# A 64-byte shift of the weight tiles against the activation tiles in SBUF, in a two-layer hybrid decoder trunk

## The chip, the cores and the metric

The kernel runs on one core of one Trainium2 chip. The metric is the device time of one execution, in microseconds (us). It is computed in float32: every large product is made from float32 operands that are split into a rounded high part and a remainder, so that one product takes three matmuls.

## The reference

One sequence of 512 tokens with 1024 features goes through two layers. Layer 0 mixes tokens with an mLSTM (8 heads), layer 1 with sliding-window attention (16 query heads, 2 key heads, window 128). Each mixer is followed by a gated MLP of width 2816.

```python
for i in range(DEPTH):                                   # 2 layers
    z = rmsnorm(h, norm_mix_pre[i])
    z = mlstm_mixer(...) if i % 2 == 0 else swa_sink_mixer(...)
    h = h + rmsnorm(z, norm_mix_post[i])
    z = conv_ffn(rmsnorm(h, norm_ffn_pre[i]), f_w_up[i], f_conv_w[i], f_conv_b[i], f_w_down[i])
    h = h + rmsnorm(z, norm_ffn_post[i])

def conv_ffn(h, w_up, conv_w, conv_b, w_down):
    gate, val = jnp.split(h @ w_up, 2, axis=-1)
    gate_c = conv_b + sum(conv_w[j] * pad(gate)[:, j:j + S] for j in range(3))
    return (jax.nn.silu(gate_c) * val) @ w_down
```

## The kernel before

**Operands.** Weights come from HBM by SyncE's queue into `raw` (4 slots of 128 x 1024 float32). ScalarE rounds a slot into `w_hi` (8 slots), VectorE writes the remainder `raw - w_hi` into `w_lo` (8 slots). Activations are kept the same way, as `act_hi` and `act_lo`. A product is then three matmuls that add up in PSUM: high by high, high by low, low by high. For each of them TensorE first loads one operand (128 x 128, the stationary one) and then streams the other (256 or 512 columns, the moving one). The load for a matmul is made while the matmul before it streams.

Which of the two is the weight depends on the stage. In `project` (lines 1803 to 1811) and in `product` (lines 2054 to 2065) the stationary operand is a weight tile and the moving one an activation. In `v_unit` (1889 to 1891), `out_part` (2000 to 2002) and `down_part` (2094 to 2096) it is the reverse. There the hidden activations of the MLP, also split in two, lie for most of the work in `hid_pair`, which is slot 2 of `w_hi` and `w_lo`; they are stationary, and slots 0 and 1 are moving.

**The MLP's first product in sevens.** Of 22 tiles of the MLP's width, 18 go through a loop in which eight half-size products are replaced by seven (a scheme like Strassen's), on sums of weights and of activations. One pass of the loop handles two tiles (t = 0 and 1); what is done for one tile is called a half pass here, and there are 36 half passes in the kernel, 18 in each layer. A half pass on TensorE is seven products of 12 matmuls with 256 columns, in this order, named by their moving operand:

- `z1a` from `act_hi`/`act_lo`; `t3` from `t_third`; `t2` from `t_early`; `t4` from `t_last`; `t1` from `t_early`; `z2a` and `z2b` from `act_hi`/`act_lo`.

Their stationary operands are forms in `w_hi` and `w_lo`. For the next tile GpSimd makes four sums of raw weights in `sums` (lines 611 to 616; `sums` lies on `w_lo`) as soon as `z2b` of the tile before this one is done (line 610). ScalarE rounds (lines 870, 872, 880), VectorE takes remainders (1517, 1520, 1533). Between the products ScalarE copies parts out of PSUM (line 892), and `t2`, `t4`, `t1` and `z2b` each wait for one of these copies, because they go on in the bank that it reads. `t2` waits for the copy of `z1a`'s result into `u_full`. That copy stands on ScalarE behind the SiLU of the tile before (line 903), and the SiLU waits for the convolution on VectorE (lines 1455, 1459). So four engines hang together in one ring of waits.

**Where the tiles lie.** Tiles are laid down one behind the other in the order in which the program names them, each on the next multiple of 32 bytes. In bytes per partition: `raw` 16384, `w_hi` 32768, `w_lo` 32768, `act_hi` 16384, `act_lo` 16384, `h` 16384, `g_post` and `g_pre` 4096 each, `arena` 65696, `ident` 512, `causal` 512, `ones` 4 (the next tile begins 32 further), `band` 1024, `u_full` 2048, `parts` 3072, `t_last` 8192. `t_early` lies 49152 bytes into `arena`, and `t_third` on `g_post` and `g_pre`. The streamed slices begin at multiples of 512 bytes within their tiles.

`freed(g)` (line 105) gives the count of used weight units for which the writer of unit `g` in a slot has to wait; it has a case of its own for slot 2, because `hid_pair` is kept there.

Of the kernel before, what the change touches and what calls it, by code (L numbers as in the profile page):

```python
# [30 lines left out]
P = 128  # L31
# [8 lines left out]
def trunk(nc, x, x_turned, columns, m_w_in, m_gate_bias, m_w_out, a_w_in, a_sinks, a_w_out,  # L40
          a_b_out, norm_mix_pre, norm_mix_post, norm_ffn_pre, norm_ffn_post, f_w_up, f_w_down, out):
    S, D = x.shape[1], x.shape[2]
# [9 lines left out]
    HALF = 512  # L52
# [19 lines left out]
    G_DOWN = [G_UP[0] + 2 * FT, 0]  # L72
    G_AIN = G_DOWN[0] + FT
    A_UNITS = (QH + 2 * KVH) * DH // P
    PLAIN = 4
    SEVENS = FT - PLAIN
    HT = S // 2
    QW = KT // 2 * P
    assert FT % 2 == 0 and PLAIN == 4
# [6 lines left out]
    SLOT = [0, 1, 2, 3, 7] + [n % 4 for n in range(QK_UNITS - FIRST + V_UNITS + O_UNITS)]  # L86
    FFN_SLOTS = [4 + n % 4 for n in range(2 * PLAIN)]
    FFN_SLOTS += [(0, 1, 6, 7)[n % 4] for n in range(2 * SEVENS)] + [n % 2 for n in range(FT - TAIL)]
    FFN_SLOTS += list(range(4, 4 + TAIL))
# [14 lines left out]

    def freed(g):
        users = [q for q in range(g) if SLOT[q] == SLOT[g]]
        if SLOT[g] == 2 and g > G_DOWN[0]:

            users.append(G_DOWN[0] + FT - TAIL - 1)
        for l in range(2):  # L110
            if g >= G_DOWN[l]:

                users.append(G_DOWN[l] - (1 if SLOT[g] >= 4 else 3))
        return counted(max(users, default=-1))
# [4 lines left out]
    with ExitStack() as ctx:  # L119
        def sb(name, shape, dt=F32):  # L120
            return ctx.enter_context(nc.sbuf_tensor(name, shape, dt))
# [4 lines left out]
        def below():  # L126
            return (nc.sbuf_base + 31) // 32 * 32
# [2 lines left out]


        raw = sb("raw", [P, 4, D])
        w_hi = sb("w_hi", [P, 8, D], F32R)
        w_lo_at = below()
        w_lo = sb("w_lo", [P, 8, D], F32R)
        sums = nc.alloc_sbuf_tensor_at("sums", [P, 2, 8, D // 2], F32, offset=w_lo_at)

        act_hi = sb("act_hi", [P, KT, S], F32R)
        act_lo = sb("act_lo", [P, KT, S], F32R)
        h = sb("h", [P, NB, D])  # L140
# [13 lines left out]
        u_rows = u_full[0:MH]  # L154
        first_part = u_full[:].rearrange("p (b t) -> p b t", b=2)
        parts = sb("parts", [P, 3, S // 2])
        t_last_at = below()
        t_last = sb("t_last", [P, 2, D], F32R)
        t_last_sum = nc.alloc_sbuf_tensor_at("t_last_sum", [P, D], F32, offset=t_last_at + 4 * D)
# [87 lines left out]
        gate_sum = arena[0:40, Q + 7 * HALF:Q + 8 * HALF]  # L247


        hid_pair = [[w[:, 2, j * HALF:(j + 1) * HALF] for w in (w_hi, w_lo)] for j in range(2)]  # L250


        raw_in = [sem(f"raw_in{i}") for i in range(4)]
# [291 lines left out]
        def _(pool):  # L545
# [56 lines left out]
            def weight_sums(l, m, t):  # L602

                up, n = G_UP[l], l * SEVENS + t - PLAIN
                gate, val = raw[:, 2 * t], raw[:, 2 * t + 1]
# [34 lines left out]
        def _(act):  # L640
# [194 lines left out]
            def ffn(l):  # L835
# [58 lines left out]
                def joined_conv(m, t):  # L894

                    n = l * SEVENS + t - PLAIN
                    f = m * 2 + t
# [1455 lines left out]
```

How the kernel before makes its waits and increments, by code:

```python
        @block.sync  # L395
# [7 lines left out]
            def load_free(g):  # L403
                last = [q for q in range(g) if SLOT[q] % 4 == SLOT[g] % 4 and DMAS[q]]
                if last:
                    sp.wait_ge(w_lo_done, counted(last[-1]))
# [12 lines left out]
                load(m, w_k[:, 2 * m:2 * m + 2, 0:HALF], raw[:, m].rearrange("p (k c) -> p k c", k=2))  # L420
            nc.sync.dma_start(g_col[:], columns[:, 0:KT]).then_inc(g_col_in, 16)
            nc.sync.dma_start(raw[:, 0, 0:HALF], m_w_in[0, 0:P, 0:HALF]).then_inc(w_first_in, 16)
            load_turned(1, 2)
            load(0, w_k[:, 1, 0:HALF], raw[:, 0, HALF:])
            for m in range(1, FIRST):
                load_turned(2 * m, 2 * m + 2)
                load_first(m)
            GC = m_w_in.shape[2] - ROWS
            sp.wait_ge(pool_done, 1)
            nc.sync.dma_start(wg[:, :, 0:MH], w_k[:, :, GC:GC + MH]).then_inc(wg_in, 16)
            nc.sync.dma_start(wg[:, :, 32:32 + MH], w_k[:, :, GC + MH:GC + ROWS]).then_inc(wg_in, 16)
            for j in range(2):
# [4 lines left out]
            nc.sync.dma_start(vecs[:], columns[:, KT:]).then_inc(vec_in, 16)  # L438
            for n in range(FIRST, QK_UNITS):
                g = g_qk(n)
                load_free(g)
                load(g, w_k[:, :, n * P:(n + 1) * P], raw[:, SLOT[g] % 4].rearrange("p (k c) -> p k c", k=KT))
            sp.wait_ge(sum_done, KT - 1)
            nc.sync.dma_start(h[:, 0], x[0, 0:P]).then_inc(x_in[0], 16)
            VC = 2 * MH * DK
```

## Time and profile before

| | |
|---|---|
| median of 3 runs | 1062.31 us (1061.8 to 1062.31) |
| the profiled execution | 1061.99 us, of which 1060.2 us are the span shown in the profile |
| TensorE (PE) busy | 1051.5 us, 99% of the span, 6822 matmuls |
| VectorE (DVE), ScalarE (ACT), GpSimd (POOL) busy | 730.1, 531.5 and 271.9 us |
| granted clock of TensorE, mean over the span | 0.999 of 2.4 GHz |
| matmuls on split operands with 256 columns | 3840: 3024 in the sevens (lines 2061 to 2063), 816 in `project` (lines 1808 to 1810) |
| of these 816 | 48 in the mLSTM's last unit, 384 in the attention's projections, 192 at the head of each MLP |
| matmuls on split operands with 512 columns | 2248: 1056 in `down_part`, 504 in `project`, 384 in `out_part`, 192 in `v_unit`, 112 in the first units and gates |

In the rows further down, PE is a matmul and PEld the load of its stationary operand. A matmul's record lasts longer than its share of the pace, since successive matmuls overlap in the array: the pace is read from start to start. In a timeline a row is the start, the length, the engine, the line, the operation and its operands (out<-in); in brackets stands the idle time before it and who ended it.

### The profile page before, as it was taken

The numbers are of one execution on the slowest core, as the hardware profiler recorded it, in microseconds if no ns is written. First come the engines' busy times: TensorE is split into PE (matmuls) and PEld (weight loads), VectorE is DVE, ScalarE is ACT, GpSimd is POOL, SyncE is SP. The second block draws the span as 40 slices with busy tenths as digits, with TensorE's granted clock in tenths as the row PEclk, the third lists the DMA queues.
The fourth block names the chain that finished last, engine by engine and source line by source line (L and its number), as shares of the span: only waits on it lengthen the run. The fifth ranks groups of instructions, "written<-read, shape, count | busy, mean of one in ns | idle before, by whom it ended". The sixth has DMA issues, their size and how long they took to land.

```text
span 1060.2 us, 18750 instructions
## 1 busy us (share of the span) xinstructions
PE 1051.5 (99%) x6822; PEld 943.5 (89%) x6822; DVE 730.1 (69%) x1013; ACT 531.5 (50%) x971; POOL 271.9 (26%) x195
## 2 busy tenths in 40 slices
PE   9999999999999999999999999999999999999997
PEld 8888888898999999988889987789999999988886
DVE  7534579588988988633366577678898898943354
ACT  6511447445565565422355367754566566542242
POOL 1000211004565565100000023300656556400000
PEclk9999999999999999999999999999999999999999
DMA  9342328233343343122272552123234334222232
GB/s 287 108 120 80 100 81 253 48 97 91 89 119 109 88 119 113 55 92 97 99 198 61 133 127 80 21 60 100 64 96 119 100 98 119 79 80 99 99 139 80
DMA packets 154828, 111.18 MB, mean 105 GB/s; under 512 B 35536, under 2 KB 140144, under 8 KB 154784
## 3 DMA queue, kind: packets, MB, share of 16 engines
q1 hardware_dynamic: 153776, 107.41, 34.5%
q0 software_dynamic: 864, 2.92, 0.9%
q8 instruction: 28, 0.46, 0.2%
q10 hardware_dynamic: 144, 0.26, 0.1%
q14 instruction: 16, 0.13, 0.0%
HBM read 106.87 MB, written 2.13 MB: 103 GB/s over the span
## 4 chain that ended last, share of the span: by engine, by line
PE 93%; DVE 4%; SPq 1%; ACT 1%; issue 1%; DMA 0%; DVEq 0%; ACTq 0%
PE ps L2061 11%; PE ps L2063 11%; PE ps L2062 11%; PE ps L2095 8%; PE ps L2096 8%; PE ps L2094 8%; PE ps L1808 6%; PE ps L1810 5%; PE ps L1809 5%; PE ps L2000 2%; PE ps L2002 2%; PE ps L2001 2%; PE ps L1889 1%; PE ps L1890 1%; PE ps L1891 1%; PE ps L2191 1%
## 5 line engine op out<-in xcount | busy, mean ns | idle before, releaser
L1808 PE MATMUL ps<-act_hi,w_hi 128*128 128x256 f32 (+1 forms) x440 | 144.8, 329 | 1.5 <-DVE act_lo L1153 1.4
L1809 PE MATMUL ps<-act_lo,w_hi 128*128 128x256 f32 (+1 forms) x440 | 142.4, 324 | 0.0
L1810 PE MATMUL ps<-act_hi,w_lo 128*128 128x256 f32 (+1 forms) x440 | 142.4, 324 | 0.0
L2061 PE MATMUL ps<-act_hi,w_hi 128*128 128x256 f32 x432 | 122.4, 283 | 0.0
L2062 PE MATMUL ps<-act_lo,w_hi 128*128 128x256 f32 x432 | 122.4, 283 | 0.0
L2063 PE MATMUL ps<-act_hi,w_lo 128*128 128x256 f32 x432 | 122.4, 283 | 0.0
L1604 DVE TENSOR_TENSOR w_lo<-raw,w_hi 128x1024 fp32r<-128x1024 f32 x32 | 39.2, 1225 | 117.0 <-ACT w_hi L952 117.0
L611 POOL TENSOR_TENSOR sums<-raw 128x512 f32<-128x512 f32 x36 | 48.3, 1341 | 262.3 <-PE ps L1810 139.6
L2095 PE MATMUL ps<-w_lo,w_hi 128*128 128x512 f32 x288 | 112.1, 389 | 0.0
L2094 PE MATMUL ps<-w_hi 128*128 128x512 f32 x288 | 112.1, 389 | 0.0
L2096 PE MATMUL ps<-w_hi,w_lo 128*128 128x512 f32 x288 | 112.1, 389 | 0.0
L653 ACT CAST w_hi<-raw 128x1024 fp32r<-128x1024 f32 x66 | 68.1, 1045 | 63.8 <-PE ps L1891 24.7
L952 ACT CAST w_hi<-raw 128x1024 fp32r<-128x1024 f32 x32 | 33.7, 1053 | 121.5 <-PE ps L2096 121.5
L1808 PEld LDWEIGHTS ps<-act_hi,w_hi 128*128 128x128 f32 x440 | 83.7, 190 | 10.5 <-DVE act_lo L1153 1.8
L1103 DVE TENSOR_TENSOR w_lo<-raw,w_hi 128x1024 fp32r<-128x1024 f32 x65 | 78.5, 1219 | 18.8 <-ACT w_hi L653 18.8
L1810 PEld LDWEIGHTS ps<-act_hi,w_lo 128*128 128x128 f32 x440 | 83.7, 190 | 6.7
L1809 PEld LDWEIGHTS ps<-act_lo,w_hi 128*128 128x128 f32 x440 | 83.7, 190 | 6.5 <-issue 0.2
L1533 DVE TENSOR_TENSOR w_lo<-sums,w_hi 128x1024 fp32r<-128x1024 f32 x72 | 87.0, 1211 | 0.0
L880 ACT CAST w_hi<-sums 128x1024 fp32r<-128x1024 f32 x72 | 75.7, 1054 | 22.3 <-POOL sums L616 22.3
L2062 PEld LDWEIGHTS ps<-act_lo,w_hi 128*128 128x128 f32 x432 | 83.0, 192 | 0.1
L2061 PEld LDWEIGHTS ps<-act_hi,w_hi 128*128 128x128 f32 x432 | 83.0, 192 | 0.1
L2063 PEld LDWEIGHTS ps<-act_hi,w_lo 128*128 128x128 f32 x432 | 83.0, 192 | 0.0
(267 smaller groups left out, 2839.6 us busy)
## 6 DMA issues: line engine op xcount, KB each, us to landing
raw<-in_f_w_up SPq DMA_DIRECT2D x88, 512.0 KB, 4.6
raw<-in_f_w_down SPq DMA_DIRECT2D x44, 512.0 KB, 3.2
raw<-in_m_w_in SPq DMA_DIRECT2D x23, 512.0 KB, 4.2
raw<-in_m_w_out SPq DMA_DIRECT2D x8, 512.0 KB, 3.3
raw<-in_a_w_in SPq DMA_DIRECT2D x16, 256.0 KB, 4.5
raw<-in_a_w_out SPq DMA_DIRECT2D x16, 256.0 KB, 4.7
h<-in_x SPq DMA_DIRECT2D x4, 512.0 KB, 7.9
h<-in_x_turned SPq DMA_DIRECT2D x3, 512.0 KB, 6.7
```

The source lines that it names most:

```text
L880: ins = nc.scalar.copy(forms_hi[t][:, fs], sums[:, t, fs])
L1103: nc.vector.tensor_tensor(w_lo[:, s], raw[:, s % 4], w_hi[:, s].bitcast(F32), ALU.subtract).then_inc(w_lo_done, 1)
L1533: ins = nc.vector.tensor_tensor(lo, sums[:, t, fs], hi.bitcast(F32), ALU.subtract)
L1808: nc.tensor.matmul(dst, uh[:, k], zh, start=(k == 0), stop=False)
L1809: nc.tensor.matmul(dst, uh[:, k], zl, start=False, stop=False)
L1810: ins = nc.tensor.matmul(dst, ul[:, k], zh, start=False, stop=(k == KT - 1))
L2061: nc.tensor.matmul(dst, uh, zh, start=(start and k == 0), stop=False, skip_group_check=not start)
L2062: nc.tensor.matmul(dst, uh, zl, start=False, stop=False, skip_group_check=not start)
L2063: ins = nc.tensor.matmul(dst, ul, zh, start=False, stop=(k == KT // 2 - 1), skip_group_check=not start)
L2094: nc.tensor.matmul(dst, hi[:, bs], w_hi[:, s, hs], start=start, stop=False)
L2095: nc.tensor.matmul(dst, hi[:, bs], w_lo[:, s, hs], start=False, stop=False)
L2096: return nc.tensor.matmul(dst, lo[:, bs], w_hi[:, s, hs], start=False, stop=stop)
```

## The change

Three small tiles are put in. `skew`, 64 bytes, lies before `w_hi`, so that `w_hi`, `w_lo` and `sums` begin 64 bytes further on. `unskew`, again 64 bytes, lies behind them, so that `act_hi`, `act_lo`, `h`, the gains and `arena` move by 128 bytes in all. `t_skew`, 64 bytes, lies before `t_last`. `hid_pair` begins 64 bytes further inside its tile than slot 2 does, and so reaches 64 bytes into slot 3; `freed` treats slot 3 as it does slot 2.

```diff
@@ -74,6 +74,7 @@
     SEVENS = FT - PLAIN
+    SKEW = 16
     HT = S // 2
...
     def freed(g):
         users = [q for q in range(g) if SLOT[q] == SLOT[g]]
-        if SLOT[g] == 2 and g > G_DOWN[0]:
+        if SLOT[g] in (2, 3) and g > G_DOWN[0]:
             users.append(G_DOWN[0] + FT - TAIL - 1)
...
         raw = sb("raw", [P, 4, D])
+        sb("skew", [P, SKEW])
         w_hi = sb("w_hi", [P, 8, D], F32R)
...
+        sb("unskew", [P, SKEW])
         act_hi = sb("act_hi", [P, KT, S], F32R)
...
         parts = sb("parts", [P, 3, S // 2])
+        sb("t_skew", [P, SKEW])
         t_last_at = below()
...
-        hid_pair = [[w[:, 2, j * HALF:(j + 1) * HALF] for w in (w_hi, w_lo)] for j in range(2)]
+        h0 = 2 * D + SKEW
+        hid_pair = [[w[:].rearrange("p s c -> p (s c)")[:, h0 + j * HALF:h0 + (j + 1) * HALF] for w in (w_hi, w_lo)]
+                    for j in range(2)]
```

## Rows read from the trace of the kernel before

**Rows 1.** The page's busy times: engine, us, share of the span, instructions.
```profile
PE 1051.5 (99%) x6822; PEld 943.5 (89%) x6822; DVE 730.1 (69%) x1013; ACT 531.5 (50%) x971; POOL 271.9 (26%) x195
```

**Rows 2.** Waits of PE: line, releaser, us in total, times, longest.
```profile
PE ps L2061 <- ACT u_full L892: 0.6, 1, 0.6
```

**Rows 3.** PE's groups by shape: count, busy us, mean ns, idle before.
```profile
L2061 PE MATMUL ps<-act_hi,w_hi 128*128 128x256 f32 x432 | 122.4, 283 | 0.0
...
L2094 PE MATMUL ps<-w_hi 128*128 128x512 f32 x288 | 112.1, 389 | 0.0
...
L1809 PE MATMUL ps<-act_lo,w_hi 128*128 128x256 f32 x272 | 77.0, 283 | 0.0
...
L2063 PE MATMUL ps<-t_last,w_lo 128*128 128x256 f32 x144 | 39.9, 277 | 0.0
```

**Rows 4.** Timeline of PE in a half pass, two stretches.
```profile
399.72 0.28 PE L2063 MATMUL ps<-act_hi,w_lo 128*128 128x256 f32 x1
...
401.88 0.28 PE L2063 MATMUL ps<-act_hi,w_lo 128*128 128x256 f32 x1
...
405.24 0.28 PE L2061 MATMUL ps<-t_last,w_hi 128*128 128x256 f32 x1
...
406.26 0.28 PE L2061 MATMUL ps<-t_early,w_hi 128*128 128x256 f32 x1
```

**Rows 5.** Timeline of PE in the MLP's second product.
```profile
499.75 0.39 PE L2094 MATMUL ps<-w_hi 128*128 128x512 f32 x1
...
501.11 0.39 PE L2094 MATMUL ps<-w_hi 128*128 128x512 f32 x1
```

**Rows 6.** Line L2063, 350 to 380 us: ns min/median/max.
```profile
L2063 PE MATMUL ps<-act_hi,w_lo x37: 283/283/284, 349.7 to 379.7; 128*128 128x256 f32 x37
L2063 PEld LDWEIGHTS ps<-act_hi,w_lo x37: 192/192/193, 350.0 to 380.0; 128*128 128x128 f32 x37
...
L2063 PEld LDWEIGHTS ps<-t_last,w_lo x12: 188/188/189, 355.0 to 376.0; 128*128 128x128 f32 x12
L2063 PE MATMUL ps<-t_last,w_lo x12: 276/277/280, 355.1 to 376.1; 128*128 128x256 f32 x12
```

**Rows 7.** L2063's matmul before PE's wait at 262.5 us.
```profile
L2063 PE MATMUL ps<-t_third,w_lo x1: 279/279/279, 262.5 to 262.5; 128*128 128x256 f32 x1
```

**Rows 8.** Line L2096, 500 to 520 us.
```profile
L2096 PEld LDWEIGHTS ps<-w_hi,w_lo x30: 187/188/188, 500.0 to 519.7; 128*128 128x128 f32 x30
L2096 PE MATMUL ps<-w_hi,w_lo x30: 389/389/390, 500.2 to 519.9; 128*128 128x512 f32 x30
```

**Rows 9.** L2096's last matmul, with no load beside it.
```profile
L2096 PE MATMUL ps<-w_hi,act_lo x1: 388/388/388, 561.9 to 561.9; 128*128 128x512 f32 x1
```

**Rows 10.** Timeline of PE in one half pass: first of `t2`, last of `z2b`.
```profile
353.44 0.28 PE L2061 MATMUL ps<-t_early,w_hi 128*128 128x256 f32 x1
...
360.44 0.28 PE L2063 MATMUL ps<-act_hi,w_lo 128*128 128x256 f32 x1
```

**Rows 11.** Timeline of DVE in the same half pass.
```profile
354.05 1.77 DVE L1520 TENSOR_TENSOR w_lo<-raw,w_hi 128x1024 fp32r<-128x1024 f32 x1 [0.35 <-ACT w_hi L872]
355.75 1.78 DVE L1517 TENSOR_TENSOR w_lo<-raw,w_hi 128x512 fp32r<-128x512 f32 x1
```

**Rows 12.** Timeline of ACT in the same half pass: two copies into `u_full`.
```profile
352.71 0.35 ACT L892 COPY u_full<-ps 128x256 f32<-128x256 f32 x1
...
362.65 0.35 ACT L892 COPY u_full<-ps 128x256 f32<-128x256 f32 x1
```

**Rows 13.** Timeline of POOL in the same half pass.
```profile
350.81 1.29 POOL L611 TENSOR_TENSOR sums<-raw 128x512 f32<-128x512 f32 x1 [3.83 <-PE ps L2063]
...
354.69 2.28 POOL L616 TENSOR_TENSOR sums<-raw,sums 128x512 f32<-128x512 f32 x1
...
360.81 1.30 POOL L611 TENSOR_TENSOR sums<-raw 128x512 f32<-128x512 f32 x1 [3.83 <-PE ps L2063]
```

**Rows 14.** DVE's groups by line.
```profile
L1604 DVE TENSOR_TENSOR w_lo<-raw,w_hi 128x1024 fp32r<-128x1024 f32 x32 | 39.2, 1225 | 117.0 <-ACT w_hi L952 117.0
...
L1493 DVE TENSOR_TENSOR arena<-t_last_sum,act_hi 128x1024 f32<-128x1024 f32 x2 | 2.4, 1224 | 0.1
```

## The prediction

> **What bounds the kernel now.** I read the page's busy times first. TensorE is busy for 1051.5 of 1060.2 us, and no other engine passes 69% [rows 1]. The list of waits gives PE hardly anything; the one wait inside the MLP's loop is 0.6 us long and happens once [rows 2]. So the time is the sum of the paces of the matmuls, and the question is what those paces are made of. I therefore took the groups by shape for the counts [rows 3] and the timeline for the pace, since records overlap and their lengths (283 and 389 ns) are not paces.
>
> From 399.72 to 401.88 us there are 18 matmuls with 256 columns on `act_hi` and `w_lo` and their like: 2.16 / 18 = 0.120 us each. From 405.24 to 406.26 there are nine on `t_last`: 1.02 / 9 = 0.1133 us each [rows 4]. The shape, type and stationary tiles are the same. What differs is where the moving operand lies. From `w_hi` to `act_hi` are 2 x 32768 bytes, a multiple of 128, and the same holds for `t_early` and `t_third`. From `w_hi` to `t_last` the sizes add up to 195776 bytes, which is 64 more than a multiple of 128. The kernel before thus already holds the experiment: 12 of the 84 matmuls of each half pass have the offset that the change gives to all, and these are quicker by 6.7 ns. Their loads are shorter too, 188 against 192 ns, and the matmul records 277 against 283 ns [rows 6]. The tile's name is not the cause of some other cost: it is written once per layer and streamed like the rest.
>
> **256 columns.** A half pass takes 10.00 us now (POOL's first sum comes at 350.81 and at 360.81 [rows 13]). With all 84 matmuls at 113.3 ns it would be 9.52 us on TensorE: 0.48 less, or 17.4 us over 36 half passes. Outside the loop 816 matmuls, three lines with 272 each [rows 3], would give 816 x 6.7 ns = 5.4 us.
>
> **512 columns.** Six matmuls from 499.75 to 501.11 us make 0.2267 us each [rows 5]. That is twice 0.1133: they go at the pace of the quick ones already, although stationary and moving operands lie 0 modulo 128 apart. Two more rows agree. Their loads take 188 ns, the undisturbed length [rows 8]. And a matmul with no load beside it takes 388 ns against 389 [rows 9], while with 256 columns the one with no load takes 279 against 283 [rows 7], and the `t_last` one, with a load beside it, 277. So I put the gain of the 2248 with 512 columns at 0. The bound on the good side by these rows is the whole effect of a load, 1 ns each (1.5 with the rounding of the records), or 3 us. On the other side the new offset could disturb what is undisturbed: at most the 6.7 ns seen at 256 columns, 15 us.
>
> The Trainium skill has a rule against the change: in "TensorE: Matmul & The Clock Gate", under "Step-by-step: what each phase is for", it says that TensorE has two independent SBUF read ports and that loading the next weights takes no bandwidth from the running matmul. By that rule the offset would be worth nothing and the time would stay at 1062.3; the pair 283 and 277 ns [rows 6] speaks against it. The same page, under "Back-to-back issue gap", gives columns / 2.4 + 2.5 ns, an estimate of 109 and 216 ns here, so that both shapes would have 11 ns above it; if what is above it were one cause for both, the 512s would gain as well.
>
> **What follows TensorE in the loop.** It can run at 9.52 us only if the ring behind it keeps up, and this is where I take something off. I follow the ring through the rows. The copy into `u_full` ends at 352.71 + 0.35 = 353.06, and `t2` may start; it starts at 353.44, so there are 0.38 us of slack [rows 10, 12]. From the start of `t2` to that of the next `z1a` are five products, 60 matmuls: 6.80 us at 113.3 ns (7.12 now); the last record ends 0.16 later, and POOL starts 0.08 after that [rows 10, 13]. POOL's four sums run from 350.81 to 354.69 + 2.28 = 356.97, 6.16 us [rows 13]. VectorE and POOL hold each other up there: L1517, half as wide as the 1225 ns subtraction [rows 14], takes 1.78 us and ends 0.56 behind POOL's last sum; L1520 takes 1.77 [rows 11]. From 356.97 VectorE has no gap longer than its own handovers until the SiLU and the next copy into `u_full`, which ends at 363.00: 6.03 us [rows 12]. With 0.05 for the handover to PE the ring is 0.05 + 6.80 + 0.16 + 0.08 + 6.16 + 6.03 = 19.28 us, and since POOL works on the tile after the next release it spans two half passes: 9.64 us each. At today's pace it comes to 9.80, under the 10.00 that TensorE needs, which agrees with the slack. So after the change I expect TensorE to wait some 0.1 us per half pass, first at `t2`, and the loop to give 36 x 0.36 = 13.0 us. The bounds are 17.4 (the ring keeps up with 9.52) and, if the two engines block each other longer than now, about 0.15 us per half pass, 5.4 us. I take the value from the rows as they stand, since no order of instructions changes.
>
> **Outside the loop.** At the head of layer 0's MLP PE already waits for ScalarE [rows 2], behind a VectorE that is busy throughout: being there earlier means waiting longer, so its 192 matmuls give 0. In layer 1 there is no such wait; I count half of 1.3 us. The attention's 384 matmuls are 2.6 us; steps of VectorE and ScalarE are interleaved, and I count 1.8. The mLSTM's 48 give 0.3. Together 2.8 us, between 0 and 5.4.
>
> **The rest of the change.** The three fillers cost nothing, as they are never touched. ScalarE, VectorE and POOL now see `raw` and `w_hi` 64 bytes apart; a VectorE subtraction with inputs 64 apart (`t_last_sum`, `act_hi`) takes 1224 ns and one with inputs 0 apart 1225 [rows 14], so 0. The wait for slot 3 is in place already: ScalarE writes the unit in slot 2 just before it and waits for the same count there. `raw`, the target of all weight transfers, does not move. If the cover of the slot-2 wait were gone, ScalarE's cast for one unit would come later once, under 2 us, with a weight queue of four slots behind it.
>
> **The sum.** 13.0 + 2.8 = 15.8 us off the profiled execution's 1061.99 gives 1046.2. The median of the runs is 0.3 above that execution, so I say 1046.5 us.
>
> **Rivals.**
> - The ring keeps up and the paces alone count: 17.4 + 3.4 outside = 20.8, 1041.5 us. For it: my handovers are rounded up. Against it: the slack of 0.38 us at `t2` is smaller than the 0.48 asked for. Chance 0.2.
> - The ring gives way little: 5.4 + 2.8, 1054 us. It needs POOL's and VectorE's blocking to grow by 0.2 us per half pass. Chance 0.12.
> - The 512s gain too, 2248 x 6.7 ns = 15.1 us on top, 1031.4 us. Against it stand 188 ns and 388 against 389 [rows 8, 9]. Chance 0.08.
> - The change does nothing, since `t_last` is quick for a reason other than its offset: 1062.3 us. Against it stands that `t_early`, written and streamed in the same way, goes at 283 ns. Chance 0.03. (It is the outcome by the Trainium skill's rule of two independent ports, named above.)
> - Slower: the pattern repeats at 256 bytes and not at 128. `t_last` lies 195776 bytes from `w_hi`, which is 192 modulo 256; after the change weights and activations lie 64 apart where weights are stationary, and `t_last` too. If only 192 is quick, `t4`'s 432 matmuls fall back to 120 ns and nothing else moves: 432 x 6.7 ns = 2.9 us, 1065.2 us. It decides as soon as fewer than one in eight of the others gains. A milder kin is that the 512s lose some 7 ns and cancel the gain. Chance 0.07 for both.
>
> **How the numbers follow.** What is described first has a chance of 0.5, with a range of its own from 1043.5 to 1050. The range for 8 in 10 reaches from the paces alone with some of the 3 us of the 512s, 1038, to the ring that gives way little, 1054. A measurement of this kernel tells 0.2%, 2.1 us, from no change. Faster: all cases but the last two, 0.90. Same: 0.04. Slower: 0.06.
>
> **What would show it.** Right: `act_hi`, `t_early` and `t_third` with 256 columns have records of 277 ns and loads of 188; L2094 keeps 389; PE gets small waits on ACT's `u_full` copy in the loop; half passes come every 9.6 us. Wrong: L2094 falls to 383 (the rival of the 512s) or rises; half passes of 9.52 without waits, or of 9.8 and more; 283 ns everywhere.

## The result and the profile after

The change makes the kernel slower. The kernel after takes 1066.45 us (median of 6 runs, 1065.77 to 1067.95), the one before 1061.92 us in the runs beside it (1061.44 to 1062.31). The ratio is 1.0045, with a 95% interval from 1.0032 to 1.0058. The forecast was 1046.5 us with a range from 1038 to 1054. Sign, size and range were all wrong.

The profiled execution of after took 1066.58 us, with a span of 1064.6 and a granted clock of 1.000. Its lines lie 6 further down: L2061 to L2063 are now L2067 to L2069, and L2094 to L2096 are L2100 to L2102. First the page's busy times, to be read beside [rows 1]:

```profile
PE 1055.8 (99%) x6822; PEld 937.4 (88%) x6822; DVE 727.0 (68%) x1013; ACT 531.6 (50%) x971; POOL 272.2 (26%) x195
```

The same number of matmuls keeps TensorE busy for 4.3 us longer. The busy times of ScalarE and GpSimd moved by 0.3 us at most, and VectorE's fell by 3.1. The waits of PE (line, releaser, us in total, times, longest) show why the ring of waits is not it: the one wait in the loop is 0.8 us, once, where it was 0.6 in [rows 2].

```profile
PE ps L2067 <- ACT u_full L898: 0.8, 1, 0.8
```

So it is the paces. PE's groups by shape, beside [rows 3] (count, busy us, mean ns, idle before):

```profile
L2069 PE MATMUL ps<-act_hi,w_lo 128*128 128x256 f32 x432 | 120.7, 279 | 0.0
...
L2100 PE MATMUL ps<-w_hi 128*128 128x512 f32 x288 | 113.7, 395 | 0.0
...
L1815 PE MATMUL ps<-act_lo,w_hi 128*128 128x256 f32 x272 | 75.9, 279 | 0.0
...
L2069 PE MATMUL ps<-t_last,w_lo 128*128 128x256 f32 x144 | 40.3, 280 | 0.0
```

`act` went from 283 to 279 ns, `t_last` rose from 277 to 280, and the 512-column group rose from 389 to 395. What line L2069 took from 350 to 380 us, beside [rows 6] (ns min/median/max), shows that the four moving operands of the loop are now all alike:

```profile
L2069 PE MATMUL ps<-act_hi,w_lo x37: 280/280/280, 350.0 to 379.7; 128*128 128x256 f32 x37
...
L2069 PE MATMUL ps<-t_early,w_lo x24: 280/280/280, 354.6 to 378.2; 128*128 128x256 f32 x24
...
L2069 PE MATMUL ps<-t_last,w_lo x12: 280/280/280, 356.0 to 376.8; 128*128 128x256 f32 x12
```

The paces come from the timeline of PE, by the starts, as in [rows 4, 5]:

```profile
398.15 0.28 PE L2067 MATMUL ps<-act_hi,w_hi 128*128 128x256 f32 x1
...
402.04 0.28 PE L2067 MATMUL ps<-act_hi,w_hi 128*128 128x256 f32 x1
...
405.22 0.28 PE L2067 MATMUL ps<-t_last,w_hi 128*128 128x256 f32 x1
...
406.28 0.28 PE L2067 MATMUL ps<-t_last,w_hi 128*128 128x256 f32 x1
```

```profile
502.15 0.39 PE L2100 MATMUL ps<-w_hi 128*128 128x512 f32 x1
...
504.25 0.40 PE L2100 MATMUL ps<-w_hi 128*128 128x512 f32 x1
```

From 398.15 to 402.04 there are 33 matmuls, 117.9 ns each, where 120 were and 113.3 were forecast. From 405.22 to 406.28 there are nine on `t_last`, 117.8 ns each, where 113.3 were. From 502.15 to 504.25 there are nine with 512 columns, 233.3 ns each, where 226.7 were.

**Where the time went.** I added up, from PE's first matmul to its last, the time from each matmul's start to the next one's, by the kind of product. Waits are in the sums.

| | before, us | after, us | difference |
|---|---|---|---|
| the sevens, 3024 | 360.8 | 357.1 | -3.7 |
| `project` with 256 columns, 816 | 100.1 | 98.6 | -1.5 |
| `down_part`, 512 columns, 1056 | 239.5 | 246.4 | +6.9 |
| `v_unit` and `out_part`, 512 columns, 576 | 137.0 | 139.0 | +2.0 |
| `project`, first units and gates, 512 columns | 142.4 | 143.3 | +0.9 |
| everything else | 73.5 | 73.5 | 0.0 |

The sum is +4.5 us before rounding; the spans differ by 4.4 and the medians by 4.5. A half pass takes 9.89 us, which is 84 x 117.8 ns: the 12 of `t_last` rise from 114.9 on average to 117.8, 35 ns, and give back a quarter of the 139 ns that the other 72 gain.

The forecast 113.3 ns do occur in the kernel after, but not for long: 70 matmuls in a row from 215.78 us, in `project` at the head of layer 0's MLP, and 23 from 261.54 us, at the start of the loop. Behind the next wait, in both places, the pace is 117.8 ns. Line L1816 from 216 to 222 us:

```profile
L1816 PE MATMUL ps<-act_hi,w_lo x18: 276/276/276, 215.9 to 221.7; 128*128 128x256 f32 x18
```

Counting stretches of 16 and more, 131 of the 3840 matmuls with 256 columns ran so.

### The profile page after: what moved, and what is told of

It reads as the page before. It is cut to its first block, busy times and chain, and to the rows that moved or that the text cites. A ratio compares the mean times of both kernels' runs of the same rounds, so it can differ in the third digit from the quotient of the medians.

```text
span 1064.6 us, 18750 instructions
## 1 busy us (share of the span) xinstructions
PE 1055.8 (99%) x6822; PEld 937.4 (88%) x6822; DVE 727.0 (68%) x1013; ACT 531.6 (50%) x971; POOL 272.2 (26%) x195
## 4 chain that ended last, share of the span: by engine, by line
PE 92%; DVE 5%; ACT 1%; SPq 1%; issue 1%; DMA 0%; DVEq 0%; ACTq 0%
PE ps L2068 11%; PE ps L2069 11%; PE ps L2067 11%; PE ps L2100 8%; PE ps L2102 8%; PE ps L2101 8%; PE ps L1814 5%; PE ps L1816 5%; PE ps L1815 5%; PE ps L2006 2%; PE ps L2008 2%; PE ps L2007 2%; PE ps L1895 1%; PE ps L1897 1%; PE ps L1896 1%; PE ps L2197 1%
## 5 line engine op out<-in xcount | busy, mean ns | idle before, releaser
L1816 PE MATMUL ps<-act_hi,w_lo 128*128 128x256 f32 (+1 forms) x440 | 141.6, 322 | 0.0
L2069 PE MATMUL ps<-act_hi,w_lo 128*128 128x256 f32 x432 | 120.7, 279 | 0.0
L2067 PE MATMUL ps<-act_hi,w_hi 128*128 128x256 f32 x432 | 120.5, 279 | 0.0
L2100 PE MATMUL ps<-w_hi 128*128 128x512 f32 x288 | 113.7, 395 | 0.0
L2102 PE MATMUL ps<-w_hi,w_lo 128*128 128x512 f32 x288 | 113.7, 395 | 0.0
L958 ACT CAST w_hi<-raw 128x1024 fp32r<-128x1024 f32 x32 | 33.6, 1049 | 126.4 <-PE ps L2102 126.4
L1814 PEld LDWEIGHTS ps<-act_hi,w_hi 128*128 128x128 f32 x440 | 82.6, 188 | 9.9 <-DVE act_lo L1159 1.3
L1816 PEld LDWEIGHTS ps<-act_hi,w_lo 128*128 128x128 f32 x440 | 82.6, 188 | 7.1
L1815 PEld LDWEIGHTS ps<-act_lo,w_hi 128*128 128x128 f32 x440 | 82.6, 188 | 6.9 <-issue 0.2
L2068 PEld LDWEIGHTS ps<-act_lo,w_hi 128*128 128x128 f32 x432 | 81.2, 188 | 0.1
L2067 PE MATMUL ps<-t_early,w_hi 128*128 128x256 f32 x288 | 80.5, 279 | 0.8 <-ACT u_full L898 0.8
L2067 PEld LDWEIGHTS ps<-act_hi,w_hi 128*128 128x128 f32 x432 | 81.0, 187 | 0.1
```

The source lines that it names most:

```text
L1814: nc.tensor.matmul(dst, uh[:, k], zh, start=(k == 0), stop=False)
L1815: nc.tensor.matmul(dst, uh[:, k], zl, start=False, stop=False)
L1816: ins = nc.tensor.matmul(dst, ul[:, k], zh, start=False, stop=(k == KT - 1))
L2067: nc.tensor.matmul(dst, uh, zh, start=(start and k == 0), stop=False, skip_group_check=not start)
L2068: nc.tensor.matmul(dst, uh, zl, start=False, stop=False, skip_group_check=not start)
L2069: ins = nc.tensor.matmul(dst, ul, zh, start=False, stop=(k == KT // 2 - 1), skip_group_check=not start)
```

## The experiments

In all of them "offset" is the place of the moving operand less that of the stationary one, in bytes modulo 256. In the kernel before it is 0 nearly everywhere and 192 for `t_last`. After the change it is 64 where a weight is stationary, and 192 (64 the other way) where a weight is moving.

**map, map2, map3: streams of matmuls alone.** The question: is the pace a function of the offset alone, with which period, and for 512 columns too? These kernels leave out the reference's computation. Each case is 48 matmuls on split operands, in groups of three as in the kernel, one case right behind the other, without waits:

```python
def stretch(a, d, n, reps, mm):      # stationary at byte a, moving at byte a + d, n columns
    sh, sl = STAT_HI + a // 4, STAT_LO + a // 4
    zh, zl = MOV_HI + (a + d) // 4, MOV_LO + (a + d) // 4
```

> Not the reference's computation: a kernel with only streams of matmuls on split operands, 48 for each of 46 cases: 256 and 512 columns, moving operand 0 to 240 bytes (steps of 16) beyond the stationary one modulo 512, and three absolute starts. It measures the disputed cost by itself. Theory A, that the offset between the operands modulo 256 sets the pace: 256 columns at 0 give 120 ns, at 64 some 118, at 192 113.3; 512 columns at 0 give 227, at 64 some 230, at 192 some 233. Theory B, that only the offset modulo 128 counts and something else disturbed the changed kernel: 64 and 192 give one pace, 113.3 ns with 256 columns and 227 with 512. Theory C, that absolute addresses count: the cases that start 64 and 128 bytes further differ from those that start at 0 with the same offset.

What map measured, as the mean from start to start over the last 24 of a case:

| offset | 0 | 16 | 32 | 48 | 64 | 80 | 96 | 112 |
|---|---|---|---|---|---|---|---|---|
| 256 columns, ns | 120.0 | 118.6 | 116.7 | 118.4 | 117.8 | 119.8 | 120.0 | 113.4 |
| 512 columns, ns | 226.7 | 231.6 | 233.3 | 233.4 | 228.7 | 231.2 | 233.1 | 231.4 |

| offset | 128 | 144 | 160 | 176 | 192 | 208 | 224 | 240 |
|---|---|---|---|---|---|---|---|---|
| 256 columns, ns | 118.5 | 118.9 | 117.3 | 119.5 | 113.4 | 119.2 | 118.4 | 117.3 |
| 512 columns, ns | 232.3 | 233.4 | 234.4 | 233.3 | 233.4 | 234.5 | 233.4 | 226.7 |

The groups by shape of map show the same in the lengths of the records. L62, L65 and L70 are the offsets 64, 112 and 192 with 256 columns, L74, L78 and L86 are 0, 64 and 192 with 512:

```profile
L86 PE MATMUL ps<-area 128*128 128x512 f32 x48 | 11.4, 395 | 0.0
...
L78 PE MATMUL ps<-area 128*128 128x512 f32 x48 | 11.2, 392 | 0.0
L74 PE MATMUL ps<-area 128*128 128x512 f32 x48 | 11.1, 390 | 0.0
...
L58 PE MATMUL ps<-area 128*128 128x256 f32 x48 | 5.9, 283 | 0.0
...
L62 PE MATMUL ps<-area 128*128 128x256 f32 x48 | 5.8, 280 | 0.0
...
L70 PE MATMUL ps<-area 128*128 128x256 f32 x48 | 5.6, 276 | 0.0
L65 PE MATMUL ps<-area 128*128 128x256 f32 x48 | 5.6, 275 | 0.0
```

So streams with nothing beside them have the paces of both kernels: 120.0 at 0, 117.8 at 64, 113.4 at 192, 226.7 at 0 and 233.4 at 192. What sign the offset has matters, since 64 and 192 are the same distance in two directions. And the two shapes want different things: with 512 columns 0 is the best there is (240 ties with it here), with 256 columns it is the worst (96 ties with it). The cases that start 64 and 128 bytes further gave the same paces within 0.4 ns, with one exception: at start 128, behind a stream at 64, offset 192 stayed at 117.7.

> Not the reference's computation: streams of matmuls only, 48 for each case. In the first such kernel offset 192 gave 113.35 ns with 256 columns at two absolute starts and 117.7 at the third, where it came behind offset 64. Theory A, absolute start: 192 gives 113.35 at starts 0, 64 and 192, and 117.7 at start 128, whatever ran before. Theory B, history: after offset 0 it is 113.35 at each start, after offset 64 it may stay at 117.7. Also 112 (113.35 expected at once), and 512 columns at 0 and 240 after other offsets (226.7 expected).

map2 changed what comes ahead of each case. At all four starts (0, 64, 128, 192) offset 192 reached 113.35 ns behind offsets 0, 64 and 128; but behind a stream of 512 columns at offset 0 it stayed at 117.7 for all 48, and behind one at 192 it was 113.35 again. Offset 0 always came back to 226.65 with 512 columns; offset 240, at 226.7 in map, gave 236.8 both times, against what was expected. Offset 192 thus has two steady paces. The offset of the stream just before does not decide alone which one comes: behind 64 it was 117.7 in map and 113.35 in all four cases of map2.

> Not the reference's computation: streams of matmuls only, 48 for each case, each case behind one at offset 0. Offsets of 256 bytes and more. If the pattern repeats at 256 bytes, then with 256 columns 256 and 512 give 120 ns like 0, 320 gives 117.8 like 64, 448 and 704 give 113.35 like 192, 368 like 112. If it repeats at 512 or 1024 only, 256, 320 and 448 give other paces.

In map3 the offsets 256, 320, 368, 448, 512 and 704 gave 120.0, 117.7, 113.4, 113.3, 120.0 and 113.3 ns with 256 columns, and 226.7, 228.9, 231.4, 233.4, 226.7 and 233.4 with 512. 256 is 0, 320 is 64, 448 is 192 and so is 704: the pattern repeats at 256 bytes.

**hid0: the changed kernel, with only the hidden activations' slices put back.**

```diff
-        h0 = 2 * D + SKEW
+        h0 = 2 * D
```

> The changed kernel with hid_pair put back on the start of slot 2, so that the 864 matmuls of the MLP's second product that read it have both operands 0 apart modulo 128 again; all else as changed. Theory A, that the 512-column matmuls lose by the offset itself: these return from 233.3 to 227 ns, 864 x 6.4 ns = 5.5 us less than the changed kernel, 1061. Rival, that they were disturbed by something else (the operands' place, or the transfers beside them): 1066.4, unchanged.

Measured: 1060.71 us (1059.88 to 1061.4, 10 runs), ratio to the kernel before 0.999 (0.9981 to 1.0), so 5.7 us less than after. L2102 from 500 to 520 us is back at the record of [rows 8]:

```profile
L2102 PE MATMUL ps<-w_hi,w_lo x30: 389/389/389, 500.2 to 519.9; 128*128 128x512 f32 x30
```

864 matmuls x 6.7 ns are 5.8 us. This one line of the change alone is worth more than the whole loss of 4.5.

**tlast0, t64, t192: the kernel before, with only `t` tiles moved.** `t_skew` (64 bytes before `t_last`) moves `t_last`; a filler behind `h` moves `t_early` and `t_third` too.

```diff
# tlast0: t_last at 0, all others as before
+        sb("t_skew", [P, 16])
# t64: all t tiles at 64
+        sb("t_gap", [P, 16])
+        sb("t_skew", [P, 16])
# t192: all t tiles at 192
+        sb("t_gap", [P, 48])
+        sb("t_skew", [P, 16])
```

> The kernel before, with 64 bytes ahead of t_last alone, so that this tile too lies 0 modulo 256 beyond the weights. Theory A: its 432 matmuls return to 120 ns, a half pass takes 10.08 us, the kernel 2.9 us more, 1064.7. Rival (the tile is quick for another reason than its offset): 1061.8, unchanged.

tlast0: 1064.99 us (1064.07 to 1066.84, 6 runs), ratio 1.0027 (1.0015 to 1.0039). All products at 120.0 ns and half passes of 10.08 us. The quick pace of `t_last` was its place and nothing else, and it was worth 2.9 us.

> The kernel before, with 64 bytes ahead of the gains and 64 ahead of t_last: t_third, t_early and t_last lie 64 modulo 256 beyond the weight forms, where the quicker kernel had them at 192; all else at 0. Modulo 128 the two kernels are the same. Theory A (modulo 256): these 48 matmuls of a half pass at 117.8 ns, 9.97 us in place of 10.00, the kernel 0.9 us less, 1061.1. Rival (modulo 128): as with 192, 1056.7.

t64: 1061.28 us (1060.35 to 1063.04, 10 runs), ratio 0.9992 (0.9982 to 1.0001). The `t` products went at 117.8 ns, a half pass at 9.98 us.

> The kernel before, with a filler of 192 bytes ahead of the gains and one of 64 ahead of t_last, so that t_third, t_early and t_last all lie 192 modulo 256 beyond the weight forms; act_hi, act_lo and hid_pair stay at 0, so no 512-column matmul changes. Theory A (offset modulo 256 sets the pace): the products t3, t2, t4, t1 run at 113.35 ns, a half pass takes 48 x 0.11335 + 36 x 0.120 = 9.76 us instead of 10.00, and the kernel 8.6 us less: 1053.3. Rival (t4's pace came from its place between other products, not from its offset): only t4 is quick, 1061.8. If the ring of engines were the limit already at 9.9, 1058.

t192: 1056.66 us (1055.93 to 1058.36, 5 runs), ratio 0.9954 (0.994 to 0.9968). t64 and t192 have the same offset modulo 128; modulo 256 they don't, and 4.6 us lie between them. t192 was expected at 1053.3 and missed that. In it half passes are mostly 9.76 us in turn with 9.86 to 10.03, 9.81 to 9.90 on average over two. In the longer ones TensorE waits at `t2` for the copy into `u_full` (PE's timeline, then ScalarE's):

```profile
371.32 0.28 PE L2065 MATMUL ps<-t_third,w_lo 128*128 128x256 f32 x1
371.43 0.37 PE L2063 MATMUL ps<-t_early,w_hi 128*128 128x256 f32 x1
371.64 0.28 PE L2064 MATMUL ps<-t_early,w_hi 128*128 128x256 f32 x1
```

```profile
371.01 0.35 ACT L894 COPY u_full<-ps 128x256 f32<-128x256 f32 x1
```

The copy ends at 371.36 and `t2` starts 0.07 later; its first matmul holds the next one up until 0.21 us after its own start, where 0.11 is the pace. Behind some of these waits `t2`, `t4` and `t1` then ran at 117.8 instead of 113.3 ns: the second pace of offset 192.

**all192 and all192b: activations and t tiles at 192, weights at 0.** The two are the same kernel, and what is said of the trace is read from that of all192b.

```diff
+        sb("act_gap", [P, 48])      # before act_hi
+        sb("t_skew", [P, 16])
```

> The kernel before, with 192 bytes between w_lo and act_hi: act_hi, act_lo and all t tiles lie 192 modulo 256 beyond the weights, hid_pair at 0. 256 columns at 113.35 ns everywhere: TensorE could do a half pass in 9.52 us. If the ring of waits is at 9.64, as the prediction worked out, the loop gives 13.0 us; if it isn't there, 17.3. Outside the loop 816 matmuls give up to 5.4; 616 in project and the first units with 512 columns lose 6.7 ns each (4.1 us), 768 with swapped roles, 64 apart, lose 2.2 ns (1.7 us). Together 1049.2 with the ring, 1045 without it. The rival that only offsets modulo 128 count gives what the changed kernel gave with hid_pair at 0, 1060.7.

> The kernel with 192 bytes between weights and activations once more, for a profile at the full clock. It took 1059 us where 1045 to 1049 had been expected. Theory R (the ring of waits): half passes of 9.7 to 9.8 us, in which PE waits at t2. Theory H (history: offset 192 has two paces, 113.35 and 117.74 ns, and a wait puts the stream into the slower): half passes with all seven products at 117.7, 9.89 us. Both would leave the loop near 1058 to 1060 in total; the paces by product tell them apart.

all192: 1059.42 us (median of 11 runs), ratio 0.9968 (0.9959 to 0.9977), where 1045 to 1049 had been expected. all192b: 1058.71 us (1058.24 to 1060.17, 7 runs), ratio 0.9965 (0.9954 to 0.9977). Line L2065 from 350 to 380 us:

```profile
L2065 PE MATMUL ps<-act_hi,w_lo x38: 281/281/281, 349.8 to 379.9; 128*128 128x256 f32 x38
...
L2065 PE MATMUL ps<-t_last,w_lo x12: 281/281/281, 355.5 to 376.3; 128*128 128x256 f32 x12
```

In this stretch all 84 of a half pass went at 117.8 ns, 9.89 us, although their offset is the one at which `t_last` makes 113.3 before. It didn't begin so. In layer 0 the products ran at 113.3 ns for three half passes, also behind the wait at the head of the loop (line L2065 from 262 to 291 us, apart from a slower start behind each wait):

```profile
L2065 PE MATMUL ps<-act_hi,w_lo x33: 276/276/276, 262.0 to 290.7; 128*128 128x256 f32 x33
```

Three waits at `t2` left them there, the fourth, at 294.4 us, put them at 117.8, and there they stayed. In layer 1 the first half pass took 9.53 us, and the wait at `t2` in the second did the same. Even the offset of `t_last`, given to all, would not have given its pace to all for long.

**map4: streams of 24, each behind a wait of another length.** Again without the reference's computation.

> Not the reference's computation: 40 streams of 24 matmuls, each behind a wait of PE for a ScalarE copy of eight widths (64 to 512 columns), so that the streams start after waits of different lengths. Offsets 0, 64, 112 and 192 with 256 columns, and 0 with 512. Theory H (offset 192 has two stable paces and the start picks one): some of the eight streams at 192 settle at 113.35 ns and others stay at 117.74, while those at 0 (120) and 64 (117.8) are the same behind every wait. Rival (a fixed pace for each offset): all eight at 192 reach 113.35, and the 117.8 of the full kernel with everything at 192 needs another cause.

Eight waits each at the offsets 0, 64, 112 and 192 gave 120.0, 117.8 and 113.3 ns in all eight for the first three; those at 112 had it from their eleventh or twelfth matmul on. At 192 six of eight settled at 117.8, two at 113.3. With 512 columns at 0 all eight gave 226.7. Records of PE by line (ns min/median/max), two lines of offset 112 and three of 192:

```profile
L92 PE MATMUL ps<-area x24: 275/275/386, 115.6 to 118.4; 128*128 128x256 f32 x24
...
L93 PE MATMUL ps<-area x24: 275/275/386, 119.5 to 122.3; 128*128 128x256 f32 x24
...
L95 PE MATMUL ps<-area x24: 281/281/385, 126.6 to 129.4; 128*128 128x256 f32 x24
...
L96 PE MATMUL ps<-area x24: 276/276/384, 130.2 to 133.0; 128*128 128x256 f32 x24
...
L97 PE MATMUL ps<-area x24: 281/281/384, 133.8 to 136.7; 128*128 128x256 f32 x24
```

281 is the slower of the two paces of 192 and 276 the faster. Offset 112 settled at one pace only, so it was tried in the kernel next. (64 did so too in these streams, and yet it has two in the kernel after, as shown above.)

**all112, map5, t112: does offset 112 carry over?** In all112 the weights (`w_hi`, `w_lo` and `sums`) were viewed 144 bytes further inside tiles that are 256 bytes longer, and `t_last` moved by 64 bytes; everything else stayed at its place modulo 256.

```diff
+        def shifted(tile):
+            return tile[:, 36:36 + 8 * D].rearrange("p (s c) -> p s c", s=8)
-        w_hi = sb("w_hi", [P, 8, D], F32R)
+        w_hi = shifted(sb("w_hi", [P, 8 * D + 64], F32R))
...      # w_lo and sums in the same way
+        sb("t_skew", [P, 16])
```

> The kernel before, with the views of w_hi, w_lo and sums begun 144 bytes further in tiles that are 256 bytes longer, and a filler of 64 bytes ahead of t_last: act_hi, act_lo and every t tile lie 112 modulo 256 beyond the weights, the one offset with 113.35 ns that no wait disturbed. It shows what the ring of waits allows when TensorE could do a half pass in 9.52 us. Outside: 816 matmuls of 256 columns give up to 5.4 us; 616 with 512 columns at 112 lose 4.7 ns each (2.9 us), 768 with swapped roles, at 144, lose 6.7 ns (5.1 us); hid_pair stays at 0. Ring as in the prediction (9.64): 1061.9 - 13.0 - 5.4 + 8.0 = 1051.5. Ring as the alternation of 9.76 and 9.88 us under t tiles at 192 suggests (12.70 us beside the five products, 9.75 per half pass): 1055.5. No ring (9.52): 1047.

all112 missed: 1073.4 us (1073.29 to 1074.55, 4 runs), ratio 1.0105 (1.0088 to 1.0122). `act` had records of 284 ns, a pace of 120, and the second product of the MLP, whose offset was 0 as before, 393:

```profile
L2068 PE MATMUL ps<-act_hi,w_lo x36: 284/284/285, 351.2 to 375.3; 128*128 128x256 f32 x36
```

```profile
L2101 PE MATMUL ps<-w_hi,w_lo x30: 393/393/393, 499.8 to 519.9; 128*128 128x512 f32 x30
```

In t112 the weights stay, and the `t` tiles are viewed 112 bytes further (all in the same way as `t_last` here); map5 asks the streams alone about the starts.

```diff
+        def shifted(tile, n):
+            return tile[:, 28:28 + n * D].rearrange("p (s c) -> p s c", s=n)
-        t_last = sb("t_last", [P, 2, D], F32R)
+        t_last = shifted(sb("t_last", [P, 2 * D + 32], F32R), 2)
...      # t_early, t_third and the sums; fillers before arena and t_last
```

> The kernel before, with only the t tiles (t_early, t_third, t_last and their sums) begun 112 bytes further modulo 256; weights, act and hid stay at offset 0, so every stationary operand starts at a multiple of 256 and only the moving operands of t3, t4, t1 and t2 differ, by 112. The change of every weight by 144 bytes in all112 gave 120 ns where the streams alone had given 113.3 for 112. Theory A (the difference of 112 is as good in the kernel as in the streams, and the weights' start at 144 spoiled all112): t2, t3, t4 and t1 at 113.3 ns, with z1a, z1b and z2a at 120 and the 512-column matmuls at 226.7; the first 8 or so of t3 slower; unlike 192, the wait at t2 does not send it into the slower pace; half passes 9.76 to 9.85 us, the kernel 1054 to 1056 us, against 1056.7 for the t tiles at 192. If the ring of waits allows no less than its 9.82 us average, 1055.5. Theory B (112 is a property of streams without anything beside them, the kernel's other engines spoil it): t products at 118 to 120 ns, t_last loses its 113.3, 1061 to 1065 us.

> Only streams of 48 matmuls, without the reference's computation; each stream comes behind one with both operands at 0. Stationary operands begin at 16, 32, 48, 96, 144, 160 or 192, the moving ones at the same place or 112 further; with 512 columns also at 144 plus 192, and two with a difference of 144 from different starts. Theory A (the start of the operands counts beside the difference, as soon as it is no multiple of 64; this spoiled all112): 120 ns for start 144 with a difference of 112, 231 for start 144 with 512 columns and a difference of 0; 113.3 for start 192 with 112. Theory B (only the difference counts and all112 lost by something else in the kernel): 113.3 for 112 at every start, 120 for 0 at every start, 226.7 with 512 columns for 0 at every start.

map5: with 256 columns and offset 112 the starts 32, 96, 160 and 192 gave 113.3 ns, the starts 16, 48 and 144 gave 120.0, 120.0 and 118.2. With 512 columns and offset 0 the starts 32, 64 and 96 gave 226.7, start 144 gave 231.1, which is the pace that all112 had in the MLP's second product. Such a start doesn't only cost: at start 144 with 512 columns, offset 112 gave 226.7 and 192 gave 228.8, where start 0 has 231.4 and 233.4 in map, and with 256 columns offset 0 gave 118.2 to 118.4 at the starts 16, 48 and 144 instead of 120.0. Groups by shape; L83 is start 144 with offset 0, L89 start 32 with offset 0, L61 start 16 and L79 start 160 with offset 112:

```profile
L83 PE MATMUL ps<-area 128*128 128x512 f32 x48 | 11.3, 393 | 0.0
...
L89 PE MATMUL ps<-area 128*128 128x512 f32 x48 | 11.1, 390 | 0.0
...
L61 PE MATMUL ps<-area 128*128 128x256 f32 x48 | 5.9, 282 | 0.0
...
L79 PE MATMUL ps<-area 128*128 128x256 f32 x48 | 5.6, 276 | 0.0
```

The offset alone decides only where operands begin at multiples of 32; at the starts tried that are odd multiples of 16, the start counts too, and this spoiled all112. Which of these starts all112 has is seen in the program as built: the kernel's tiles begin with `raw` at byte 4224, so weights and activations lie at 128 modulo 256, and not at 0 as the expectation of t112 has it (map and map2 gave start 128 the paces of start 0); the weights of all112 lie at 16. For start 16 with offset 112 the streams gave 120.0, and so did the kernel. (No stream had 512 columns at start 16.)

t112: 1056.25 us (1056.13 to 1056.72, 5 runs), ratio 0.9942 (0.9928 to 0.9955). It has the lowest median of all versions, 10.2 us below the kernel after, though it is not told apart from t192 or from act112 below. `t4` and `t1` went at 113.3 ns in all but one of the 36 half passes. `t3`, behind 0, needed all its 12 matmuls to get there (118.3), and `t2` was at 113.3 or, mostly in every second half pass, at 118.6 to 120.0; half passes are mostly 9.81 and 9.88 us in turn.

**act112: the t tiles of t112, and `act_hi` and `act_lo` 112 bytes further too.** The first kernel in which TensorE asks for the forecast 9.52 us, and so the test of the ring term.

```diff
+        def act_tile(name):
+            return sb(name, [P, KT * S + 64], F32R)[:, 28:28 + KT * S].rearrange("p (k s) -> p k s", k=KT)
+        act_hi = act_tile("act_hi")
+        act_lo = act_tile("act_lo")
```

> The t tiles as in t112, and act_hi and act_lo begun 112 bytes further modulo 256 as well; weights and hid stay at 0. All 84 matmuls of a half pass then have the difference of 112, which in the streams gave 113.3 ns. This is the first kernel in which TensorE asks for half passes of 9.52 us, as the prediction thought of the change itself, so it tests its term for the ring of waits. The 512-column matmuls with an activation on one side lose: 616 of project at 231.4 against 226.7, 768 of the others at 233.3, 8.0 us in all; hid stays at 226.7. Outside the loop the 256-column ones give about 2.8 us. Theory P (the prediction's ring arithmetic, 9.64 us per half pass): 13.0 us in the loop, the kernel 1054.2 us. Theory K (the ring keeps up with 9.52): 1049.9 us, no waits. Theory L (the ring is longer than the prediction's sum; pairs of half passes were never under 19.62 us in the version with the t tiles at 192, where TensorE waited at t2): half passes of 9.8 us with a wait at t2, 6.5 to 7 us in the loop, 1060 to 1061 us.

Measured: 1056.76 us (1056.07 to 1057.25, 5 runs), ratio 0.9948 (0.9935 to 0.9962). The time lies between those of theories P and L, and none of the three named it. Inside the loop all products but `t2` run at 113.3 ns once the head is past. TensorE now waits at `t2` in most half passes, and two of them together take 19.47 to 19.55 us in layer 0, some 9.75 each (in layer 1, 9.52 and 10.04 to 10.06 in turn, 9.78). PE's timeline at such a wait, and ScalarE's copy:

```profile
384.86 0.28 PE L2074 MATMUL ps<-t_third,w_lo 128*128 128x256 f32 x1
385.05 0.38 PE L2072 MATMUL ps<-t_early,w_hi 128*128 128x256 f32 x1
385.27 0.28 PE L2073 MATMUL ps<-t_early,w_hi 128*128 128x256 f32 x1
```

```profile
384.64 0.36 ACT L903 COPY u_full<-ps 128x256 f32<-128x256 f32 x1
```

The copy ends at 385.00, `t2` starts 0.05 later, as the prediction had it; but its second matmul comes only 0.22 us behind the first, and the next seven to ten follow at 114 to 121 ns. The other thing this kernel shows is at the head of the loop. TensorE waits 2.21 us there (its first matmul behind the wait starts at 266.47), against 0.6 before, and then its clock falls. Busy time and granted clock of PE in stretches (us, busy with count, clock, DMA share, GB/s):

```profile
264.00:266.00 2.00, 0.27 (x3) 1.00 0.16 46
266.00:267.00 1.00, 0.53 (x4) 1.00 1.06 316
267.00:268.00 1.00, 1.00 (x11) 1.00 1.16 344
268.00:269.00 1.00, 1.00 (x7) 0.50 1.14 280
269.00:270.00 1.00, 1.00 (x6) 0.50 0.14 34
270.00:271.00 1.00, 1.00 (x7) 0.50 0.00 0
271.00:272.00 1.00, 1.00 (x9) 0.79 0.00 0
```

From 268.0 to 271.4 us the clock is at 0.50, its lower level of 1.2 GHz, and a matmul takes 213 ns instead of 113. The first half pass took 13.7 us, 4.2 above 9.52: 2.4 in the wait and most of the rest in the clock. By kind, against before: the sevens -5.7 us, `project` with 256 columns -3.8, `down_part` +1.2, the other 512s +3.5; sum -4.8, as the spans have it.

## Why the prediction was wrong

**What bounds the kernel.** Right. TensorE's paces set the time before and after, and every experiment's time follows from counts times paces, with waits added.

**The 256-column term: the step that failed.** The prediction said that `t_last` "is 64 more than a multiple of 128" away and so "has the offset that the change gives to all". It took the row's difference in pace (120 and 113.3 ns, which stands) and gave it a modulus that no row supported. The offset of `t_last` is 192 modulo 256, what the change gives is 64. map shows 113.4 ns for the one and 117.8 for the other, map3 that the period is 256, t64 and t192 the same within the kernel. The row of `t_last` was also a best case: its nine matmuls had settled, its 12 take 114.9 ns on average. So 2592 of the loop's matmuls gained 2.2 ns or less where 6.7 were booked, and `t_last` lost. The term "36 x 0.36 = 13.0 us" measured 3.7, and the 2.8 us outside the loop 1.5. The prediction knew this case: it worked out 192 modulo 256 in its last rival, and gave it 0.07 together with its kin. Nothing in the trace spoke for 128 over 256, so they should have had like chances. A second premise was silent: that a place has one pace. 64 did run at 113.3 ns in 131 matmuls of the kernel after, and 192, given to all in all192b, ended at 117.8; the right modulus alone would not have saved the term.

**The 512-column term: mis-sized, and the loss came from here.** The gain was put at 0 and a loss of up to 6.7 ns each named as the bound on the bad side. It was nearly the bound: where nothing else holds them up, the 1056 of `down_part` and the 576 of `v_unit` and `out_part` rose from 226.7 to 233.3 ns, those of `project` by 2.2. Over all of them, waits included, it is 6.5, 3.4 and 1.5 ns each; together 9.8 us where 0 stood. The argument for 0 was that these matmuls are undisturbed at offset 0 (188 and 389 ns, [rows 8]). That was right, and map agrees: 226.7 is the least of all 16 offsets. But what is undisturbed could only lose from a move, and a loss was left out of the sum. hid0 shows the mechanism in the kernel: 864 of them put back gave 5.7 us.

**The Trainium skill's rule.** "TensorE: Matmul & The Clock Gate", in "Step-by-step: what each phase is for", says that the two SBUF read ports are independent and that loading the next weights takes no read bandwidth from the running matmul. By it the offset would be worth nothing. Here the same instructions take 113.3 to 120.0 ns, and 226.7 to 236.8, by where the one operand lies against the other; the measurements decide against that consequence, and where in the chip the two meet no run shows. The same page's formula under "Back-to-back issue gap", which it gives for the isolated matmul (an estimate of 109 and 216 ns here), was not reached by any offset.

**The ring.** Never reached by the change: after it TensorE asks for 9.89 us, and the ring's 9.8 at such a pace is below that. act112 tested it. The prediction's 9.64 us per half pass measured 9.75 to 9.78. It had the right place (`t2`, for ScalarE's `u_full` copy) and nearly the right length. The piece it left out: a product that starts behind a wait is slower at first. From `t2` to the next `z1a` it took 6.94 to 6.96 us with a wait ahead, where 60 x 113.3 ns = 6.80 were booked. The rest of the ring, 19.49 - 6.96 = 12.53 us over two half passes, was 12.48 in the sum. With all at 113.3 ns the loop would thus have given 8 to 9 us and not 13.0, less some 3.4 at its head if the wait there grows as in act112 (the first half pass was 0.8 us over its usual length in the kernel before and 4.2 in act112); that exposure was priced for the matmuls ahead of the wait (0 gain) but not for the clock behind it.

**The rest.** Fillers, the wait for slot 3 and the 64 bytes between the inputs of the other engines cost nothing: everything else in the table of kinds is 73.5 us in both, and VectorE's busy time did not rise.

**The rivals.** What happened is both halves of the last rival at once, a period of 256 and the 512s losing some 7 ns; each was named, but as alternatives, and the second as something that would "cancel the gain" of a change that otherwise works. The rivals for it had 0.07. That the first half's figure, 1065.2 us, lies near the measured 1066.45 is luck: in it `t4` fell back to 120 ns and nothing else moved, where in fact `t4` went to 117.8, the other 256-column matmuls gained, and most of the loss came with 512 columns. The check "L2094 rises" was named as the sign of a wrong forecast, and it was.

## What to carry to other kernels

A pace read at one offset says only that this offset is quick; before it is given to others, ask which moduli fit (here 128, 256 and every larger power of two did) and give each a share of the chances. Both shapes of a kernel need their own price: what is best for 512 columns here (0) is the worst for 256, and the two best offsets for 256 (112 and 192) cost 4.7 and 6.7 ns with 512. The change moved both because it moved the tile that they share; moving the small operands that only the loop reads (t112, t192) gave 5 to 6 us with the same trick. And a faster engine doesn't keep its gain across a wait: it pays at the restart, and a longer wait can cost it its clock.

## What the runs showed of the hardware

These hold for split float32 operands (fp32r), 128 rows and a new stationary operand for each matmul, at full clock:

- The pace depends on the moving operand's place less the stationary one's, modulo 256 bytes: 113.3 to 120.0 ns with 256 columns, 226.7 to 236.8 with 512. The direction counts (64: 117.8, 192: 113.4, both in map).
- That holds for starts at multiples of 32; at the three odd multiples of 16 that were tried (16, 48, 144), offset 112 did not reach 113.3 ns, and with 512 columns at start 144 it gave 226.7 instead of 231.4.
- Some offsets have two steady paces, chosen by how the stream is entered. 192 ran at 113.3 or 117.8 ns for dozens of matmuls, in streams alone and in the kernel, and some waits switched it (all192b, t192). 64 did the same in the kernel after (113.3 for 70 matmuls in a row), though no stream showed it. 512 columns at offset 240 gave 226.7 in map and 236.8 in map2.
- The first matmul behind a wait takes up to 0.22 us to the next one's start instead of 0.11 (0.220 to 0.227 in map4 with 256 columns, 0.14 to 0.22 in the kernels).
- Behind a wait of 2.21 us, from 1.5 us after the restart, the granted clock was 0.50 for 3.4 us (act112). Behind waits of 0.6 us (before) and 0.8 us (after) in the same place it stayed at 1.00.

Left open: what in the memory makes the pattern, why 112 takes up to 11 matmuls to settle behind offset 0 and about as many again behind a wait, what picks one of two paces at a wait, and whether a place that is good for both shapes exists; at none of the 16 offsets of map was 113.3 ns met by 226.7.
